# Readout of the first state space model: products over 128 rows first, products over 64 rows with the halves in turns

## The chip, the cores and the metric

The kernel runs on one core of one Trainium2 chip. The metric is the device time of one execution in microseconds (us); lower is better. The engines are TensorE (PE, with its weight loads shown as PEld), VectorE (DVE), ScalarE (ACT), GpSimd (POOL) and SyncE (SP), which issues most of the DMA transfers.

## The reference

Three blocks in a row on a sequence of 1024 positions with 1024 channels, all in f32: a block with stick-breaking attention and a convolution, a block with pooling and sliding-window attention, and a block with two state space models. The change lies in the third block, in the first of its two models (`s5_branch`): 64 groups of 16 channels, each with 64 complex states that decay independently.

```python
def step(h0, uc):
    bu = jnp.einsum('btgh,gnh->btgn', uc, B_bar)
    a = jnp.broadcast_to(A_bar, bu.shape)
    _, local = lax.associative_scan(combine, (a, bu), axis=1)
    states = local + pows * h0[:, None]
    y = jnp.einsum('btgn,ghn->btgh', states, Cc).real
    return states[:, -1], y
```

The output then gets `D * u` added, goes through a gelu, a gate by a projection of itself (`w_glu`) and a gate by `z_s5`, and is joined with the second model's output in `w_out`.

## The kernel before

Each engine has one program, written out in order; a small book of names turns `w.wait_ge(name, ...)` into waits on semaphores. Large products are made from f32 operands split into a high and a low part (`mm3`, lines 561 to 563, three products each). Their weights come in by SP (`load_raw`, line 3458), ScalarE makes the high part (L1218) and GpSimd the low part (L3214).

The first state space model takes 8 positions together, so that a sequence of 1024 is 128 chunks of 8. The work goes by eight blocks of 128 channels, e_ = 0 to 7 (called groups here). A block holds 8 groups of 16 channels of the reference. For each of them there is a table of 128x128 that gives the part of the output from the inputs of the same chunk, and two tables of 64x128 (real and imaginary part) that give the part from the state ahead of the chunk. The tables were made earlier, lie in DRAM, and are loaded into one of two places (`tab5`), even and odd blocks in turns.

PE's program per block, from `tensor_program`:

- `uproj(e_ + 1, e_, ...)`: the projection of the next block's inputs (L561 to L563), this block's gate projection, and the transposes (L567) that lay the next block's inputs out by chunk (`UG`).
- `results(e_)`, the readout, lines 1141 to 1155. Per half hf of the partitions it takes a PSUM bank of two (`ybk`), waits for the tables (`tab_s`, `tab_a`) and for the states (`h5`), and makes four tiles of 128 columns. Each tile is the sum of three products: the chunk's own inputs over 128 rows (L1152), the real part of the state over 64 rows (L1153) and the imaginary part over 64 rows (L1154). Half 0 uses partitions 0 to 63 of the states and their tables, half 1 partitions 64 to 127. Each half signals `y5_ps` at its end.
- `mid(e_ + 1)`: the inputs to the next block's states (L1137).
- `turned5(e_)`: transposes of the readout (L567).

Block 7 has its readout and its transposes later, behind the first quarter of the output projection (`wo(0, 0, 0)`), with nothing between them.

Who is waiting on the readout: ScalarE applies the gelu to each half's bank (`back5`, L2064), and the transposes wait for both. SP's `load_t(e_ + 2)` (L3629 for the tables, L3631 for four of the eight pieces of the 128x128 table) and ScalarE's (L1994, the other four) wait for `y5_ps` of half 1, since they load into the place that the readout has just used; SP issues the next weights behind that. `load_t(1)` alone is issued earlier, during block 0's projections. The states come from `mid` on VectorE and GpSimd: ScalarE copies L1137's result (L2057), VectorE multiplies (L3075 on), scans, and ends with L3101, which signals `h5`. ScalarE's L2006 evacuates the input projection; in ScalarE's program it stands behind an L1218.

Of the kernel before, what the change touches and what calls it, by code (L numbers as in the profile page):

```python
# [226 lines left out]
def build(nc, ap, out):  # L227
    ctx = ExitStack()
    with ctx:
# [4 lines left out]
        psum = ctx.enter_context(nc.psum_tensor("psum", [128, 8, 512], F32))  # L234
# [7 lines left out]
        def view(at, *shape):  # L242

            a = int(round(at * KB))
            n = 1
            for x in shape:
                n *= x
            v = arena[:, a:a + n]
            if len(shape) == 2:
                v = v.rearrange("p (a b) -> p a b", a=shape[0])  # L250
            elif len(shape) == 3:
                v = v.rearrange("p (a b c) -> p a b c", a=shape[0], b=shape[1])
            return v

        def half_of(half):
            return slice(512 * half, 512 * half + 512)

        def tile_of(tile):
            return slice(128 * tile, 128 * tile + 128)
# [257 lines left out]
        UG = [view(48, 8, 128), view(52, 8, 128)]  # L517
        Wr5, Wi5, Gr5, Gi5 = view(56, 4, 128), view(58, 4, 128), view(60, 4, 128), view(62, 4, 128)
        Hr5, Hi5, Xa5, Xb5 = view(64, 4, 128), view(66, 4, 128), view(68, 4, 128), view(70, 4, 128)
# [5 lines left out]
        def tab5(e_):  # L525

            a = T_AT[e_ % 2]
            t = view(a, 6, 4, 128)
            return [view(a, 8, 64), view(a + 2, 8, 64)], [t[:, q] for q in range(2, 6)], view(a + 12, 8, 128)
# [11 lines left out]
        def tensor_program(e, w):  # L541
# [4 lines left out]
            def take(ring, key, *freed):  # L546

                bank, before = ring.turn(*freed)
                book.bank_of[key] = bank
                for event in before:  # L550
                    w.wait_ge(*event)
                return bank
# [12 lines left out]
            def tp(o, in_):  # L565
                n = in_.shape[0]
                return e.transpose(o, in_, ident[0:n, 0:n])  # L567
# [301 lines left out]
            for g in range(4):  # L869
                run(proj_cm("u2_ps", (g,), w2, 256 * g, 2, pb, lambda m, half: [("u2", g, m, half)]))  # L870
                run(proj_cm("z2_ps", (2 * g,), w2, 4096 + 256 * g, 2, pb, lambda m, half: [("z2", 2 * g, m, half)]))
                for m in range(2):
                    for half in range(2):
                        bank = take(pb, ("pool_ps", g, m, half), ("pool", g, m, half))
# [3 lines left out]
                        for kb in range(2):  # L878
                            t = e.matmul(psum[:, bank, :], WP[:, kb, 128 * m:128 * m + 128], PL[:, kb, half_of(half)],  # L879
                                         start=kb == 0, stop=kb == 1)  # L880
# [17 lines left out]
            for m in range(8):  # L898
                run(proj_cm("q2_ps", (m,), w2, 128 * m, 1, pb, lambda _, half: [("q2", m, half)]))
                if m == 0:  # L900
                    for hf in range(2):
                        bank = take(pb, ("v2_tp", hf), ("v2", hf))
                        w.wait_ge("v2c", hf)
                        for j in range(4):
                            t = tp(psum[:, bank, tile_of(j)], V2T[:, tile_of(4 * hf + j)])
# [91 lines left out]
            for half in range(2):  # L997
                bank = take(pbk, ("dt_tp", half), ("dt_add", half))
                w.wait_ge("dt_c", half)
                for k in range(4):  # L1000
                    t = tp(psum[:, bank, tile_of(k)], DTF[half][:, tile_of(k)])
# [3 lines left out]
            bank = take(sb, ("dt_acs",), ("dt_dec_in",), ("dt_et",))  # L1005
# [77 lines left out]
            p5k, ubk, wbk, ybk = Banks(free_bank, [0, 1]), Banks(free_bank, [2, 3]), Banks(free_bank, [4, 5]), Banks(free_bank, [6, 7])  # L1083
# [56 lines left out]

            def results(e_):
                _, (car, cai, _, _), TG = tab5(e_)
                for hf in range(2):
                    lo = 64 * hf
                    bank = take(ybk, ("y5_ps", e_, hf), ("ys", e_, hf))
                    w.wait_ge("tab_s", e_)
                    w.wait_ge("tab_a", e_)
                    w.wait_ge("h5", e_)
                    w.wait_ge("h5_z", 1)
                    for k in range(4):  # L1150
                        ps = psum[:, bank, tile_of(k)]
                        e.matmul(ps, UG[e_ % 2][:, 2 * k + hf, :], TG[:, 2 * k + hf, :], start=True, stop=False)  # L1152
                        e.matmul(ps, Hr5[lo:lo + 64, k, :], car[lo:lo + 64, k, :], start=False, stop=False)  # L1153
                        t = e.matmul(ps, Hi5[lo:lo + 64, k, :], cai[lo:lo + 64, k, :], start=False, stop=True)  # L1154
                    t.then_inc(*w.up("y5_ps", e_, hf))

            def turned5(e_):
                for hf in range(2):
# [10 lines left out]
            for e_ in range(7):  # L1169
                uproj(e_ + 1, e_, lambda: e_ or step("sum", 3, 1, Banks(free_bank, [7])))  # L1170
                results(e_)
                mid(e_ + 1)
                turned5(e_)
# [5 lines left out]
            for half in range(2):  # L1179
                for ch in range(2):  # L1180
                    wo(0, half, ch, pb if half else Banks(free_bank, [2, 3, 6, 7] if ch else [0, 1, 4, 5]))
                    if half + ch == 0:
                        results(7)
                        turned5(7)
# [9 lines left out]
            for ch in range(2):  # L1194
                r = book.raw_of.get(("ple", ch), 0)
                wt = raw(r, 2, 512)
                for tile in range(8):
                    bank = take(pb, ("pp_ps", ch, tile), ("pp", ch, tile))
                    w.wait_ge("raw", r)
                    w.wait_ge("pt3")  # L1200
                    for kb in range(2):
                        t = e.matmul(psum[:, bank, :], PT3[:, kb, tile_of(tile)], wt[:, kb, :], start=kb == 0, stop=kb == 1)  # L1202
# [2572 lines left out]
```

## Time and profile before

| | |
|---|---|
| time, median of 3 runs | 3140.32 us (3138.95 to 3142.75) |
| span of the profiled execution, first to last instruction | 3139.1 us |
| PE busy | 3048.2 us (97%), 15412 instructions |
| DVE, ACT, POOL busy | 1650.6, 1155.6, 964.1 us |
| mean granted TensorE clock | 0.991 of full speed |

The profile is of one execution, and its times count from the span's start. Its span is 1.2 us below the median of the runs. PE's instructions overlap: the start of one to the start of the next says what it costs, its own duration includes what runs beneath its neighbours.

### The profile page before, as it was taken

The numbers are of one execution on the slowest core, as the hardware profiler recorded it, in microseconds if no ns is written. First come the engines' busy times: TensorE is split into PE (matmuls) and PEld (weight loads), VectorE is DVE, ScalarE is ACT, GpSimd is POOL, SyncE is SP. The second block draws the span as 40 slices with busy tenths as digits, with TensorE's granted clock in tenths as the row PEclk, the third lists the DMA queues.
The fourth block names the chain that finished last, engine by engine and source line by source line (L and its number), as shares of the span: only waits on it lengthen the run. The fifth ranks groups of instructions, "written<-read, shape, count | busy, mean of one in ns | idle before, by whom it ended". The sixth has DMA issues, their size and how long they took to land.

```text
span 3139.1 us, 38243 instructions
## 1 busy us (share of the span) xinstructions
PE 3048.2 (97%) x15412; PEld 2443.9 (78%) x15412; DVE 1650.6 (53%) x2710; ACT 1155.6 (37%) x1971; POOL 964.1 (31%) x700
## 2 busy tenths in 40 slices
PE   8999989999999999999999999999999999999998
PEld 7876658887878888777888756778778878788877
DVE  6989661025546654233243587666655555533436
ACT  3125553222341121113332286445546323332334
POOL 2220002233417785124522122411111233342523
PEclk9999989999999999999999999999999999999999
DMA  4110001112422233113332210421011243443323
GB/s 137 47 36 19 14 14 47 48 54 108 135 62 86 86 105 95 44 47 134 108 116 61 56 55 28 161 76 34 22 47 48 92 110 94 141 139 109 108 74 108
DMA packets 252657, 243.75 MB, mean 78 GB/s; under 512 B 15776, under 2 KB 198048, under 8 KB 251456
## 3 DMA queue, kind: packets, MB, share of 16 engines
q1 hardware_dynamic: 231536, 197.10, 21.0%
q10 hardware_dynamic: 20944, 44.21, 4.3%
q8 instruction: 122, 2.00, 0.3%
q14 instruction: 55, 0.45, 0.0%
HBM read 200.83 MB, written 38.73 MB: 76 GB/s over the span
## 4 chain that ended last, share of the span: by engine, by line
PE 84%; DVE 6%; ACT 4%; DMA 3%; issue 1%; POOL 1%; SPq 1%; ACTq 0%; DVEq 0%
PE psum L561 23%; PE psum L563 23%; PE psum L562 23%; PE psum L567 3%; DMA arena<-in_w_in 2%; PE psum L744 1%; PE psum L770 1%; DVE arena L2915 1%; PE psum L1202 1%; PE psum L1153 1%; PE psum L1152 1%; PE psum L934 1%; ACT WS L1218 1%; PE psum L879 1%; PE psum L958 1%
## 5 line engine op out<-in xcount | busy, mean ns | idle before, releaser
L3214 POOL TENSOR_TENSOR WS<-arena,WS 128x1024 fp32r<-128x1024 f32 x279 | 692.7, 2488 | 1729.2 <-ACT WS L1218 1729.1
L561 PE MATMUL psum<-XH,WS 128*128 128x512 f32 x2600 | 1031.9, 397 | 16.2 <-ACT arena L2006 3.5
L563 PE MATMUL psum<-XH,WS 128*128 128x512 f32 x2600 | 1015.6, 391 | 0.0
L562 PE MATMUL psum<-XL,WS 128*128 128x512 f32 x2600 | 1014.9, 390 | 0.0
L561 PEld LDWEIGHTS psum<-XH,WS 128*128 128x128 f32 x2600 | 489.2, 188 | 134.3 <-issue 13.8
L563 PEld LDWEIGHTS psum<-XH,WS 128*128 128x128 f32 x2600 | 489.0, 188 | 103.5
L562 PEld LDWEIGHTS psum<-XL,WS 128*128 128x128 f32 x2600 | 489.5, 188 | 96.7 <-issue 0.7
L1218 ACT ACTIVATE WS<-arena 128x1024 fp32r<-128x1024 f32 x279 | 293.0, 1059 | 730.9 <-PE psum L563 255.3
L561 PE MATMUL psum<-WS,XH 128*128 128x512 f32 x960 | 378.1, 394 | 7.2 <-POOL WS L3214 5.1
L562 PE MATMUL psum<-WS,XH 128*128 128x512 f32 x960 | 374.9, 391 | 0.0
L563 PE MATMUL psum<-WS,XL 128*128 128x512 f32 x960 | 374.8, 390 | 0.0
L561 PEld LDWEIGHTS psum<-WS,XH 128*128 128x128 f32 x960 | 180.7, 188 | 53.4 <-issue 7.4
L563 PEld LDWEIGHTS psum<-WS,XL 128*128 128x128 f32 x960 | 180.7, 188 | 37.8
L562 PEld LDWEIGHTS psum<-WS,XH 128*128 128x128 f32 x960 | 180.8, 188 | 36.8 <-issue 0.2
L2241 DVE TENSOR_TENSOR XL<-arena,XH 128x512 fp32r<-128x512 f32 x86 | 85.7, 1052 | 206.1 <-ACT XH L1271 206.1
L567 PE MATMUL psum<-arena 128*128 128x128 f32 x1152 | 164.1, 282 | 21.3 <-DVE arena L2817 9.5
L2331 DVE SCALAR_TENSOR_TENSOR arena<-arena 128x1024 f32<-128x1024 f32 x120 | 180.3, 1502 | 3.4
L567 PEld LDWEIGHTS psum<-arena 128*128 128x128 f32 x1152 | 132.8, 146 | 53.3 <-issue 29.0
L3298 POOL TENSOR_TENSOR arena<-arena 128x8 f32<-128x8 f32 (+7 forms) x320 | 153.9, 508 | 60.4 <-DVE arena L2549 52.9
L2549 DVE TENSOR_TENSOR arena<-arena 128x64 f32<-128x64 f32 (+5 forms) x188 | 115.0, 651 | 63.4 <-ACT arena L1605 32.2
L2376 DVE TENSOR_TENSOR_SCAN arena<-arena 128x128 f32<-128x128 f32 (+7 forms) x64 | 93.2, 1456 | 43.2 <-ACT arena L1407 43.1
L2915 DVE SCALAR_TENSOR_TENSOR arena<-arena 128x512 f32<-128x512 f32 x96 | 81.8, 852 | 51.9 <-ACT arena L1937 49.2
(304 smaller groups left out, 3075.2 us busy)
## 6 DMA issues: line engine op xcount, KB each, us to landing
arena<-in_w_in SPq DMA_DIRECT2D x85, 512.0 KB, 3.8
arena<-in_w_out SPq DMA_DIRECT2D x48, 512.0 KB, 3.5
arena<-in_w_in_even SPq DMA_DIRECT2D x48, 512.0 KB, 4.3
arena<-in_w_out_even SPq DMA_DIRECT2D x32, 512.0 KB, 3.6
h_spill<-arena ACTq DMA_DIRECT2D x24, 512.0 KB, 3.1
arena<-s_table SPq DMA_DIRECT2D x8, 1536.0 KB, 6.8
arena<-in_w_in_odd SPq DMA_DIRECT2D x18, 512.0 KB, 3.9
s_table<-arena SPq DMA_DIRECT2D x32, 256.0 KB, 3.0
```

Of the source, the lines that this page charges most:

```text
L561: e.matmul(ps, wh, xh, start=start, stop=False)
L562: e.matmul(ps, wh, xl, start=False, stop=False)
L563: return e.matmul(ps, wl, xh, start=False, stop=stop)
L567: return e.transpose(o, in_, ident[0:n, 0:n])
L1218: e.activation(split_hl(u, kbs, n)[0], raw(r, kbs, n), ACT.Copy).then_inc(*w.up("w_hi", u))
L2241: e.tensor_tensor(XL[:, kb, half_of(half)], src(kb)[:, half_of(half)], XH[:, kb, half_of(half)].bitcast(F32), SUB).then_inc(*w.up("x_lo_v" ...
L2331: e.scalar_tensor_tensor(o, c[:, k:k + S], col("conv_w", 31 * m + k), o, M, A_).then_inc(*w.up("conv", m, k))
L2376: e.tensor_tensor_scan(q[:, ::-1], q[:, ::-1], zero.broadcast_to([128, nk]), 1.0, M, A_).then_inc(*w.up("att_scan", k, h))
L2549: e.tensor_tensor(o, a, b, op).then_inc(*w.up("tbv", *key, also=also))
L2915: e.scalar_tensor_tensor(o, R[:, k:k + 512], col("conv_w_3", 16 * k + cb), o, M, A_).then_inc(*w.up("cv_k", g, i, half, k, also=[("cv_c", ...
L3214: e.tensor_tensor(lo, raw(book.raw_of.get(("w", u), 0), kbs, n), hi.bitcast(F32), SUB).then_inc(*w.up("w_lo", u))
L3298: e.tensor_tensor(o, a, b, op).then_inc(*w.up("tbp", *key, also=also))
```

## The change

In the readout, both banks are taken at the start, and the eight products over 128 rows of both halves come first, waiting only for the tables. Of the products in a bank the first alone carries `start`. Then come the wait for the states and the sixteen products over 64 rows: per tile, first the real and then the imaginary part, each for half 0 and half 1 in turn. Both halves signal at the end, with the last two products. The number and the operands of the products are as before.

```diff
             def results(e_):
                 _, (car, cai, _, _), TG = tab5(e_)
+                banks = [take(ybk, ("y5_ps", e_, hf), ("ys", e_, hf)) for hf in range(2)]
+                w.wait_ge("tab_s", e_)
+                w.wait_ge("tab_a", e_)
                 for hf in range(2):
-                    lo = 64 * hf
-                    bank = take(ybk, ("y5_ps", e_, hf), ("ys", e_, hf))
-                    w.wait_ge("tab_s", e_)
-                    w.wait_ge("tab_a", e_)
-                    w.wait_ge("h5", e_)
-                    w.wait_ge("h5_z", 1)
                     for k in range(4):
-                        ps = psum[:, bank, tile_of(k)]
-                        e.matmul(ps, UG[e_ % 2][:, 2 * k + hf, :], TG[:, 2 * k + hf, :], start=True, stop=False)
-                        e.matmul(ps, Hr5[lo:lo + 64, k, :], car[lo:lo + 64, k, :], start=False, stop=False)
-                        t = e.matmul(ps, Hi5[lo:lo + 64, k, :], cai[lo:lo + 64, k, :], start=False, stop=True)
-                    t.then_inc(*w.up("y5_ps", e_, hf))
+                        e.matmul(psum[:, banks[hf], tile_of(k)], UG[e_ % 2][:, 2 * k + hf, :], TG[:, 2 * k + hf, :],
+                                 start=k == 0, stop=False)
+                w.wait_ge("h5", e_)
+                w.wait_ge("h5_z", 1)
+                for k in range(4):
+                    for h, ca in ((Hr5, car), (Hi5, cai)):
+                        for hf in range(2):
+                            lo, last = slice(64 * hf, 64 * hf + 64), k == 3 and h is Hi5
+                            t = e.matmul(psum[:, banks[hf], tile_of(k)], h[lo, k, :], ca[lo, k, :], start=False, stop=last)
+                            if last:
+                                t.then_inc(*w.up("y5_ps", e_, hf))
```

## Rows read from the trace of the kernel before

**Rows 1.** The page's chain that ended last, shares of the span by engine.

```profile
PE 84%; DVE 6%; ACT 4%; DMA 3%; issue 1%; POOL 1%; SPq 1%; ACTq 0%; DVEq 0%
```

**Rows 2.** Groups by line and form: count, busy us, mean ns, idle before.

```profile
L1153 PE MATMUL psum<-arena 64*128 64x128 f32 x128 | 31.1, 323 | 0.0
```

**Rows 3.** Timeline of PE, first readout: start us, duration us, instructions merged by line.

```profile
2494.35 1.03 PE L567 MATMUL psum<-arena 128*128 128x128 f32 x8
2495.22 0.39 PE L1152 MATMUL psum<-arena 128*128 128x128 f32 x2
2495.54 0.49 PE L1153 MATMUL psum<-arena 64*128 64x128 f32 x2
2495.86 0.39 PE L1154 MATMUL psum<-arena 64*128 64x128 f32 x2
2496.18 0.49 PE L1152 MATMUL psum<-arena 128*128 128x128 f32 x2
2496.60 0.48 PE L1153 MATMUL psum<-arena 64*128 64x128 f32 x2
...
2503.57 1.97 PE L1137 MATMUL psum<-arena 128*64 128x128 f32 x32
```

**Rows 4.** Chain of waits behind the third readout: start us, share of the chain, what.

```profile
2576.07 0.55 SPq L3631
...
2578.85 9.36 DMA arena<-in_w_in
...
2589.83 0.50 PE psum L561
```

**Rows 5.** Timelines of VectorE and of PE ahead of the third readout.

```profile
2557.51 2.87 DVE L3101 TENSOR_TENSOR arena<-arena 128x508 f32<-128x508 f32 x1
...
2566.38 1.03 PE L567 MATMUL psum<-arena 128*128 128x128 f32 x8
```

**Rows 6.** Timeline of PE, attention scores of the second block, halves in turns.

```profile
1795.84 1.16 PE L934 MATMUL psum<-arena 64*128 64x128 f32 x16
1796.93 0.50 PE L561 MATMUL psum<-XH,WS 128*128 128x512 f32 x1
...
1798.52 0.71 PE L934 MATMUL psum<-arena 64*128 64x128 f32 x8
```

**Rows 7.** Timeline of PE, making of the tables, halves in turns, 16-column weights.

```profile
961.66 1.92 PE L853 MATMUL psum<-arena 64*16 64x128 f32 x32
```

**Rows 8.** Table of group 1: last issue in SP's timeline; that issue's time to landing.

```profile
2493.46 0.61 SPq L3631 DMA_DIRECT2D arena<-k_table  x1
...
DMA to landing us min/median/max: 8.9/8.9/8.9
```

**Rows 9.** Timeline of PE, first half of the gate projection after the first readout.

```profile
2518.72 0.50 PE L561 MATMUL psum<-XH,WS 128*128 128x512 f32 x1 [1.25 <-ACT arena L2006]
```

**Rows 10.** PE timeline, then two stretches: engines' busy us, granted clock, DMA share, GB/s.

```profile
2739.19 0.50 PE L561 MATMUL psum<-WS,XH 128*128 128x512 f32 x1 [2.31 <-POOL WS L3214]
...
2740.80:2744.10 3.30, 3.30 (x10) 2.56 (x9) 1.66 (x1) 1.06 (x1) 1.55 (x2) 0.50 0.68 219
960.00:1215.00 255.00, 254.88 (x1334) 208.81 (x1333) 143.99 (x174) 48.35 (x71) 200.51 (x350) 1.00 0.33 96
```

**Rows 11.** Timeline of ScalarE around the first readout.

```profile
2499.72 0.60 ACT L2064 ACTIVATE arena<-psum 128x512 f32<-128x512 f32 x1
2503.68 0.60 ACT L2064 ACTIVATE arena<-psum 128x512 f32<-128x512 f32 x1 [3.37 <-PE psum L1154]
2504.71 0.60 ACT L2057 ACTIVATE arena<-psum 128x512 f32<-128x512 f32 x1 [0.44 <-PE psum L1137]
```

**Rows 12.** Timelines of PE and ScalarE, readout of group 7.

```profile
2757.26 0.38 PE L1152 MATMUL psum<-arena 128*128 128x128 f32 x2
2766.45 1.06 PE L567 MATMUL psum<-arena 128*128 128x128 f32 x8 [0.78 <-ACT arena L2064]
...
2765.71 0.60 ACT L2064 ACTIVATE arena<-psum 128x512 f32<-128x512 f32 x1 [3.63 <-PE psum L1154]
```

## The prediction

> **What bounds the kernel now.** I read the page first. TensorE (PE) makes up 84% of the chain that ended last [rows 1], so the question is what the change does to PE's own time. Line 1153, one of the two 64-row lines that the change touches, has 128 matrix instructions [rows 2]: 8 groups with 8 products each and two instructions to a product. The code gives lines 1152 and 1154 as many.
>
> Then the timeline of PE for the first readout [rows 3]. The readout runs from 2495.22 to 2503.57, when the next group's L1137 begins: 8.35 us for 24 products, 0.35 us each. The transposes ahead of it, which have the same 128x128x128 shape, start every (2495.22 - 2494.35) / 8 = 0.109 us an instruction, so 0.22 us a product. The excess sits where the row count changes: the two instructions of L1152 take 0.32 us up to L1153 (0.42 in the second round, 2496.18 to 2496.60), L1153 takes 0.32 and L1154 0.32, though the two lines of 64 rows do each no more than half of the work of L1152. PE does not stand idle in there; it is slow between forms.
>
> Does the readout lie on the path? The chain of waits in the loop over groups says yes: when a readout ends, SP issues the tables and weights for later groups, the weights land 9.36 us after their issue, and PE's second projection half begins at 2589.83 behind them [rows 4]. All of that starts at the readout's end, as does PE's own next work. The other input of a readout, the state from VectorE, is early: its last operation ends at 2557.51 + 2.87 = 2560.38, the readout starts at 2566.38 + 8 x 0.109 = 2567.25 [rows 5]. Both hang on the previous readout's end by unchanged work, so these 6.9 us of slack stay. Moving the wait for that state behind the 8 full products therefore gains nothing and costs nothing.
>
> **The change part by part.** The 8 full products together: 16 instructions x 0.109 [rows 3] = 1.74 us. Entering the 64-row form once: 0.32 - 0.22 = 0.10 us [rows 3].
>
> The 16 products of 64 rows, now with the two halves in turns into two banks: the trace of before has this pattern in the attention scores of the second block, same 64x128 weights and 128 columns [rows 6]. There 16 instructions begin at 1795.84 and the next form begins at 1796.93, so 1.09 us with the way out included; a block of 8 lasts 0.71 and one of 16 lasts 1.16, so 8 more cost 0.45 (0.056 each, about half of 0.109). For 32 instructions: 1.09 + 2 x 0.45 = 1.99 us. Bounds: the same alternation with 16-column weights and with sums of two products as here runs 32 instructions in 1.92 us [rows 7], last duration included, where my price gives 1.16 + 0.90 = 2.06: 0.14 less at the cheap end. At the dear end the halves don't overlap and each instruction takes 0.109 as a full one does: 32 x 0.109 + 0.2 = 3.7 us. I take 1.99, since its rows agree in shape. Sending `start` once per bank instead of four times changes a flag; L1152 (with it, first round) and L1154 (without) both take 0.32 [rows 3], so zero. Taking both banks ahead waits for the second gelu of the group before, which ended before that group's transposes.
>
> New readout: 1.74 + 0.10 + 1.99 = 3.83 us, a gain of 8.35 - 3.83 = **4.52 us** each (4.66 to 2.8 by the bounds). Six of the eight, groups 1 to 6, give this in full: 27.1 us. The other two don't.
>
> Group 0. After its readout PE runs L1137 of group 1, which needs that group's table. The last piece is issued by SP at 2493.46 and lands 8.9 us later [rows 8], at 2502.36, and its issue does not depend on the readout. Now L1137 starts at 2503.57 and never waits; after the change PE would be there at 2495.22 + 3.83 = 2499.05 and waits till about 2502.5: 1.07 us of the 4.52 remain. Behind the waiting L1137 on PE stand group 0's transposes and the next projection, which move with it; ScalarE's copies and the chain of group 1's states begin with it too and keep their slack to the next readout. The wait then relieves another: in this round PE waited 1.25 us for an evacuation that stood behind the weights' landing [rows 9], and those weights are asked for up to 4.5 us earlier (less, as the queue is still full). I take the whole 1.2; 0 is the other end. Against it stands the clock: after PE's idle stretch of 2.31 us before 2739.19 the granted clock was 0.50 from 2740.80 to 2744.10 [rows 10], half of full speed (1.2 GHz), which costs half of 3.30, 1.65 us. The new wait of 3.2 us is longer, so I charge 1.5 (0 to 3.3, two such stretches). Group 0 nets 1.07 + 1.2 - 1.5 = 0.8 us (-2.2 to 2.3).
>
> Evacuation. Both banks now finish together, where the first gelu used to run beneath the second half [rows 11]. A gelu takes 0.60 us. In groups 0 to 6 two in a row (1.2 us) fit beneath L1137, whose 32 instructions last 1.97 us [rows 3], so the transposes behind them are not held up; the copy of L2057 would begin at 2503.68 + 1.2 = 2504.88 in place of 2504.71, inside the 6.9 us of slack. In group 7 nothing lies between: the transposes began at 2766.45, right behind the second gelu of 2765.71 [rows 12]. New: 2757.26 + 1.74 + 0.10 + 2.06 = 2761.16, two gelus to 2762.40, transposes at 2762.54 (the 0.14 of before kept). Gain 3.9 us instead of 4.5.
>
> The Trainium skill (TensorEngine Tiling, PSUM Bottleneck) says that tiling speeds up the products but not the emptying of the banks, which may become the limit. If that held for every group, 0.6 us more would be lost in seven of them, 4.2 us in all, an estimate from the page's rule and the gelu's row. The rows side with it for group 7 alone.
>
> Sum: 27.1 + 0.8 + 3.9 = **31.8 us**. The span of the profiled execution is 3139.1, and 3107.3 would be left. The median of the runs, 3140.3, stands 1.2 above that span, so the prediction is 3108.5 us. Whether the half-clock stretch at 2740.80 comes again after the shift is open, 1.65 us either way.
>
> **Rivals.**
> No overlap, only fewer changes of form: the halves go one after the other at 0.109. Readout 1.74 + 0.10 + 3.7 = 5.5, gain 2.8: 6 x 2.8 = 16.8, group 7 some 2.2, group 0 some 2.3 (its wait is then 1.7 us and I charge no clock), 21 us, **3119 us**. Against it stand both blocks in turns [rows 6, 7]. Chance 0.07.
>
> Each change of half costs what a change of form costs, so the edit does not do what it says: 32 instructions at 0.21, the pace of L1152 behind a change in [rows 3] (0.42 for two), give 6.7; readout 1.74 + 0.10 + 6.7 + 0.2 = 8.7, about 0.4 more than before; with the late gelu of group 7 some 4 us in all, **3144 us**. The attention scores speak against it [rows 6]. The Trainium skill (TensorEngine Tiling, Key Properties) says that a change of tiling mode drains the engine and a change of tile alone does not; by that rule this case is out, and the trace agrees (0.056 us an instruction [rows 6]). Chance 0.05.
>
> Slower: the clock. With half of the rows active in short blocks the chip could count the readout as rest and grant half clock behind it, in each group. An instruction's time doubles, so half of the stretch is lost; the 4.0 us that a group gains on average are gone once the half clock lasts 8 us a group. At twice that, 16 us, it costs 8 - 4 = 4 us a group, 32 in all: **3172 us**. For it: clock drops of 3.3 us exist [rows 10]. Against it: in the 255 us that hold all eight table blocks of 64 rows in turns the granted clock is 1.00 [rows 10]. Chance 0.03.
>
> **How the numbers follow.** The forecast has 0.85; its own range is 3104 (all of group 0's relief, no clock loss, no drop at 2740) to 3113 (group 0 at its worst, a dearer pair). The full range, 3103 to 3117, leaves out the three rivals and some of the forecast's tails, together under 0.2. A difference of 0.2%, 6.3 us, is about what a measurement of this kernel can tell from none. Faster by more: forecast and first rival, 0.92. Within: the second rival, 0.05. Slower: 0.03.
>
> **What would show it.** Right: the 8 full products some 1.7 us in a row, 32 instructions of 64 rows in pairs over some 2.0 us, a readout of 3.8 in groups 1 to 6; in group 0 PE idle ahead of L1137 for about 3 us, released by a table load; in group 7 two gelus one behind the other and PE waiting about 1.3 us for them. Wrong: pairs that don't overlap; the round of a group shortened by less than its readout, with a new PE wait behind a weight load or the state; a granted clock below 1.00 in groups 1 to 6.

## Result and the profile after

The changed kernel takes 3111.26 us (median of 4 runs, 3107.21 to 3113.56) against 3140.76 beside it: ratio 0.9904, 95% interval 0.9892 to 0.9916. Run again beside three of the experiments it took 3107.43 us, ratio 0.9892 (0.9875 to 0.9908). Forecast were 3108.5 us, 3103 to 3117.

The span of the profiled execution is 3108.1 us, 31.0 less than before. PE still makes up most of the chain that ended last. DMA and SP, which stood in the chain of the group loop before [rows 4], have shrunk in it, from 3% to 2% (DMA) and from 1% to 0% (SPq). The page's chain, by engine:

```profile
PE 85%; DVE 7%; ACT 4%; DMA 2%; issue 1%; POOL 1%; SPq 0%; ACTq 0%; DVEq 0%
```

The readout of group 1, in PE's timeline (start us, duration us, instructions merged by line; L1148 is the full product, L1156 the 64-row product, L1137 the next group's first work):

```profile
2532.02 1.95 PE L1148 MATMUL psum<-arena 128*128 128x128 f32 x16
2533.90 2.06 PE L1156 MATMUL psum<-arena 64*128 64x128 f32 x32
2535.89 1.97 PE L1137 MATMUL psum<-arena 128*64 128x128 f32 x32
2537.78 1.09 PE L567 MATMUL psum<-arena 128*128 128x128 f32 x8
```

It takes 2535.89 - 2532.02 = 3.87 us where it took 8.35 [rows 3]; the groups 1 to 6 all have this within 0.01. The 32 instructions of 64 rows last 2.06 us, to the hundredth what was worked out from the attention scores [rows 6].

Group 0, PE's timeline again:

```profile
2496.36 1.03 PE L567 MATMUL psum<-arena 128*128 128x128 f32 x8
2497.23 1.95 PE L1148 MATMUL psum<-arena 128*128 128x128 f32 x16
2499.11 2.06 PE L1156 MATMUL psum<-arena 64*128 64x128 f32 x32
2504.06 3.50 PE L1137 MATMUL psum<-arena 128*64 128x128 f32 x32 [2.89 <-issue]
2507.49 1.09 PE L567 MATMUL psum<-arena 128*128 128x128 f32 x8
```

PE stands idle for 2.89 us ahead of L1137. The profile names no engine as releaser ("issue"), but the last piece of group 1's table, issued at 2495.50 (2495.5 in the line's summary below), lands 8.5 us later, so at 2504.0, and L1137 starts at 2504.06:

```profile
L3634 SPq DMA_DIRECT2D arena<-k_table x1: 599/599/599, 2495.5 to 2495.5; - x1
...
DMA to landing us min/median/max: 8.5/8.5/8.5
```

L1137 then takes 2507.49 - 2504.06 = 3.43 us and not 1.89 as in group 1, because its stretch has the granted clock at half (0.50, the number behind the engines' busy times; the stretch after it has 1.00):

```profile
2504.00:2507.20 3.20, 3.14 (x30) 3.17 (x32) 0.00 (x0) 0.60 (x1) 0.00 (x0) 0.50 1.03 321
2507.30:2524.00 16.70, 16.70 (x82) 13.85 (x79) 14.25 (x18) 4.97 (x6) 10.33 (x6) 1.00 0.67 128
```

Group 7, timelines of PE and of ScalarE (L2067 is the gelu):

```profile
2730.17 1.95 PE L1148 MATMUL psum<-arena 128*128 128x128 f32 x16
2732.05 2.06 PE L1156 MATMUL psum<-arena 64*128 64x128 f32 x32
2735.36 1.06 PE L567 MATMUL psum<-arena 128*128 128x128 f32 x8 [1.26 <-ACT arena L2067]
...
2734.13 1.08 ACT L2067 ACTIVATE arena<-psum 128x512 f32<-128x512 f32 x2 [0.98 <-PE psum L1156]
```

Both gelus now run one behind the other after the readout, and PE waits 1.26 us for them where it waited 0.78 [rows 12]. From the readout's start to the transposes it is 2735.36 - 2730.17 = 5.19 us, 9.19 before.

All waits of PE in the stage, from 2495 to 2740 (waiter, releaser: us in total, times, longest):

```profile
PE psum L1137 <- issue: 2.9, 1, 2.9
PE psum L561 <- POOL WS L3217: 2.3, 1, 2.3
PE psum L561 <- ACT arena L2009: 2.2, 2, 1.6
PE psum L567 <- ACT arena L2067: 1.3, 1, 1.3
PE psum L561 <- DVE arena L3112: 0.8, 1, 0.8
```

The first is the new one. The wait on ScalarE's evacuation (L2009, L2006 before) fell from 3.5 us in six times to 2.2 in two; the 1.25 us of group 0's round [rows 9] are gone.

Where the time went, by starts of the readouts in the two traces: the round of group 0 (first readout to second) 36.35 to 34.79 us, a gain of 1.6; the six rounds of groups 1 to 6 (second readout to the last) 225.7 to 198.2, 27.5; from the last readout on 4.0. Together 33.1 us. The first readout of the profiled execution after begins 2.0 us later than before (2497.23 against 2495.22): 1.2 us of that are there within the first 16 us, the rest comes in later stages, none of which the change touches; hence 31.0 in the spans.

### The profile page after: what moved, and what is told of

The parts are those of the page before. It is cut to its first block, busy times and chain, and to the rows that moved or that the text cites. A ratio compares the mean times of both kernels' runs of the same rounds, so it can differ in the third digit from the quotient of the medians.

```text
span 3108.1 us, 38242 instructions
## 1 busy us (share of the span) xinstructions
PE 3014.0 (97%) x15412; PEld 2423.2 (78%) x15412; DVE 1649.9 (53%) x2710; ACT 1154.8 (37%) x1971; POOL 962.6 (31%) x700
## 4 chain that ended last, share of the span: by engine, by line
PE 85%; DVE 7%; ACT 4%; DMA 2%; issue 1%; POOL 1%; SPq 0%; ACTq 0%; DVEq 0%
PE psum L561 24%; PE psum L563 23%; PE psum L562 23%; PE psum L567 4%; PE psum L744 1%; PE psum L770 1%; DVE arena L2918 1%; DMA arena<-in_w_in 1%; PE psum L1205 1%; PE psum L934 1%; PE psum L879 1%; PE psum L958 1%; PE psum L750 1%; ACT WS L1221 1%; PE psum L1025 1%
```

## The experiments

A change of form, below, is a step from products over 128 rows to products over 64 rows or back. The first three kernels are set beside the trace of the changed kernel from the result; the changed kernel was not timed again beside them.

**Halves in a row: the turns taken out.** The changed kernel with the loops exchanged.

```diff
-                for k in range(4):
-                    for h, ca in ((Hr5, car), (Hi5, cai)):
-                        for hf in range(2):
+                for hf in range(2):
+                    for k in range(4):
+                        for h, ca in ((Hr5, car), (Hi5, cai)):
```

> The changed kernel, but the 64-row products go half after half (eight of half 0, then eight of half 1), so that no two halves stand in turns; the full products still come first. Both causes: a change of form costs about 0.2 us and a 64-row instruction without its partner of the other half takes 0.109 us in place of 0.056. Then the readout takes 1.88 + 32 x 0.11 + 0.2 = 5.6 us in groups 1 to 6 where the changed kernel has 3.87, and the whole is about 11 us slower than the changed kernel, some 3122 us (group 0 gets its clock back). Rival, fewer changes of form are everything (0.28 us each): readout 3.9 us, no difference. Rival, the turns are everything and changes of form cost nothing: readout 8.3 us, about 27 us slower, as the kernel before.

Measured: 3117.75 us, ratio 0.9926 (0.9910 to 0.9943). PE's timeline of group 1's readout:

```profile
2533.45 1.95 PE L1148 MATMUL psum<-arena 128*128 128x128 f32 x16
2535.33 3.50 PE L1156 MATMUL psum<-arena 64*128 64x128 f32 x32
2538.76 1.97 PE L1137 MATMUL psum<-arena 128*64 128x128 f32 x32
```

2538.76 - 2533.45 = 5.31 us, so neither rival holds: without turns 8.35 - 5.31 = 3.04 us of the gain are there, and the turns bring 5.31 - 3.87 = 1.44 us more. The 5.6 expected were 0.3 too many, and the seam, where half 0 ends and half 1 begins, shows why. The counts below are the 64-row matrix instructions that run in a stretch ahead of the seam, across it and behind it (busy and count of PE, of PEld, then granted clock, DMA share, GB/s):

```profile
2535.40:2536.70 1.30, 1.30 (x12) 1.30 (x13) 1.00 0.00 0
2536.70:2537.20 0.50, 0.50 (x10) 0.50 (x9) 1.00 0.00 0
2537.20:2538.50 1.30, 1.30 (x16) 1.30 (x13) 1.00 0.06 13
```

An instruction lasts 0.27 us and starts every 0.112 here, so a stretch of 0.50 us would touch (0.50 + 0.27) / 0.112, about 7; it touches 10. About three instructions of half 1 run beside the last ones of half 0: the engine begins on half 1 before all of half 0 has started. In the trace's own starts the instruction that signals the end of half 0, the 16th of the block in the program, is the 19th to start. This overlap is worth 3 x 0.112 = 0.3 us and belongs to the turns, so that about 2.7 us of the 4.48 come from fewer changes of form and about 1.8 from running the halves beside each other.

From the first readout to the end this kernel takes 619.1 us where the changed kernel has 610.8: 8.3 us more, about 11 expected. One part of what was expected did not come: group 0 does not get its clock back. PE idles for 1.40 us ahead of L1137, and the clock behind it is half again (last row, columns as above for all five engines):

```profile
2505.41 3.07 PE L1137 MATMUL psum<-arena 128*64 128x128 f32 x32 [1.40 <-issue]
...
2506.20:2509.40 3.20, 3.20 (x27) 2.87 (x24) 0.09 (x1) 1.20 (x2) 0.00 (x0) 0.50 1.01 360
```

**A change of form per tile: the full products not ahead.** The turns stay, the two full products go back to their tile.

```diff
-                for hf in range(2):
-                    for k in range(4):
-                        e.matmul(psum[:, banks[hf], tile_of(k)], UG[e_ % 2][:, 2 * k + hf, :], TG[:, 2 * k + hf, :],
-                                 start=k == 0, stop=False)
                 w.wait_ge("h5", e_)
                 w.wait_ge("h5_z", 1)
                 for k in range(4):
+                    for hf in range(2):
+                        e.matmul(psum[:, banks[hf], tile_of(k)], UG[e_ % 2][:, 2 * k + hf, :], TG[:, 2 * k + hf, :],
+                                 start=k == 0, stop=False)
```

> The halves in turns as in the changed kernel, but the full products not ahead: per tile two full products, then four of 64 rows in turns, so eight changes of form in place of two. Both causes: 16 x 0.109 + 32 x 0.056 + 8 x 0.2 = 5.1 us a readout, 1.25 us more than the changed kernel, some 7 to 9 us slower, about 3119 us. Rival, changes of form are everything (0.28 each): 5.6 us. Rival, the turns are everything: 3.9 us, no difference.

Measured: 3117.40 us, ratio 0.9927 (0.9913 to 0.9942). PE's timeline, the first two of four rounds and the end:

```profile
2533.94 0.61 PE L1150 MATMUL psum<-arena 128*128 128x128 f32 x4
2534.48 0.71 PE L1155 MATMUL psum<-arena 64*128 64x128 f32 x8
2535.12 0.71 PE L1150 MATMUL psum<-arena 128*128 128x128 f32 x4
2535.77 0.71 PE L1155 MATMUL psum<-arena 64*128 64x128 f32 x8
...
2538.99 1.97 PE L1137 MATMUL psum<-arena 128*64 128x128 f32 x32
```

The readout takes 5.05 us, 5.1 expected. Six changes of form more than in the changed kernel cost 5.05 - 3.87 = 1.18 us, 0.20 each. At that price the 14 changes by which the kernel before exceeds the changed one make 2.8 us, beside the 2.7 found above. A block of four full instructions takes 0.65 us (2535.12 to 2535.77) where 4 x 0.112 = 0.45 would do: the price is paid at the edges of each block, as read ahead of the change [rows 3]. Two other readings of it fall away. It is not the `start` flag, which is sent here as in the changed kernel; and it is not the adding of one product after another into the same tile, which the halves in a row do for real and imaginary part at 0.112 us an instruction.

From the first readout to the end it takes 618.7 us, 7.9 more than the changed kernel, 7 to 9 expected. In group 0 PE idles for 1.31 us ahead of L1137, and here the clock behind it stays at 1.00:

```profile
2507.20 1.97 PE L1137 MATMUL psum<-arena 128*64 128x128 f32 x32 [1.31 <-issue]
...
2507.20:2510.40 3.20, 3.20 (x42) 2.99 (x43) 0.40 (x1) 1.20 (x2) 0.08 (x1) 1.00 1.06 361
```

**Turns of two products.** The loops over `hf` and over the real and imaginary part exchanged.

```diff
-                    for h, ca in ((Hr5, car), (Hi5, cai)):
-                        for hf in range(2):
+                    for hf in range(2):
+                        for h, ca in ((Hr5, car), (Hi5, cai)):
```

> The changed kernel with the halves in turns of two products (real and imaginary part of half 0, then of half 1). If an instruction overlaps only with the one that stands right beside it, seven of the boundaries pair: about 0.7 us saved against the 5.6 us of halves in a row, readout 4.9 us. If the engine looks past the next product to the other half, the pairs stay and the readout takes 3.9 us, no difference to the changed kernel (3111 us).

Measured: 3109.67 us (two runs), ratio 0.9902 (0.9882 to 0.9922).

```profile
2530.85 1.95 PE L1148 MATMUL psum<-arena 128*128 128x128 f32 x16
2532.73 2.16 PE L1156 MATMUL psum<-arena 64*128 64x128 f32 x32
2534.82 1.97 PE L1137 MATMUL psum<-arena 128*64 128x128 f32 x32
```

The readout takes 3.97 us, 3.9 expected for an engine that looks past the next product; the block lasts 2.16 us where the changed kernel has 2.06. So turns of two pair as well as turns of one but for 0.1 us. With the seam above (about three instructions in a block of 16) that bounds the reach here: two products yes, eight no.

**The changed kernel again**, unedited, beside the three experiments that follow.

> The changed kernel itself, timed beside the next three on one chip. 3111 us, group 0's L1137 waiting 2.9 us for its table and half clock for 3.4 us behind it.

Measured: 3107.43 us (3106.76 to 3108.42), ratio 0.9892 (0.9875 to 0.9908). The readouts take 3.87 us again, and the wait ahead of L1137 in group 0 comes again with half clock behind it (the row from 2502.70 in the next experiment).

**Table ahead of the store.** In SP's program, the table of group 1 ahead of the last store of the second model.

```diff
                         store_y(2)
-                        store_y(3)
+                        for k in range(2):
+                            w.wait_ge("y_nrm", 3, k)
                         load_t(1)
+                        store_y(3)
```

> The changed kernel, with the table of group 1 issued ahead of the store of the last group of the second model (y_spill, 1 MB) in SP's queue, not behind it. If the new wait in group 0 is for the table's landing behind that store, the table lands some 2 us earlier, the wait falls from 2.9 to about 1 us, and the half-clock stretch of 3.4 us behind it (1.5 us) goes with it: 2 to 3.5 us faster than the changed kernel. Rival, the store isn't what holds the table (the issue of its pieces is): wait and time as in the changed kernel. Rival, the clock drop doesn't come from the wait: the wait shrinks and the half clock stays.

Measured: 3108.35 us (3106.09 to 3109.64), the changed kernel beside it 3107.43 (3106.76 to 3108.42): by time, nothing, where 2 to 3.5 us were expected. By trace the step does what it should. The pieces of the table land 6.4 to 7.2 us after their issue, not 8.5 as the last one in the changed kernel, and L1137 doesn't wait at all (1 us was expected to remain):

```profile
2500.99 2.06 PE L1156 MATMUL psum<-arena 64*128 64x128 f32 x32
2503.01 1.97 PE L1137 MATMUL psum<-arena 128*64 128x128 f32 x32
2505.30 1.06 PE L567 MATMUL psum<-arena 128*128 128x128 f32 x8 [0.31 <-ACT arena L2067]
```

Group 0's round takes 31.94 us where the changed kernel beside it has 34.75: 2.8 gained. The granted clock there is 1.00. But this execution has half clock in two other stretches, which the changed kernel's execution beside it does not have. First this kernel, then the changed one, same columns as above with all five engines:

```profile
2502.50:2505.90 3.40, 3.09 (x48) 2.74 (x47) 0.00 (x0) 3.12 (x5) 0.00 (x0) 1.00 1.15 388
2711.60:2714.60 3.00, 3.00 (x9) 2.35 (x8) 2.12 (x1) 0.94 (x1) 1.57 (x1) 0.50 0.57 188
2735.50:2738.50 3.00, 2.91 (x7) 2.36 (x8) 2.59 (x4) 0.00 (x0) 0.00 (x0) 0.50 0.35 97
```

```profile
2502.70:2505.80 3.10, 3.02 (x29) 3.04 (x31) 0.00 (x0) 0.60 (x1) 0.00 (x0) 0.50 1.08 318
2711.60:2714.60 3.00, 2.85 (x12) 2.37 (x13) 3.00 (x2) 0.00 (x0) 2.91 (x2) 1.00 0.55 174
2735.50:2738.50 3.00, 2.66 (x12) 2.23 (x13) 2.89 (x5) 0.00 (x0) 0.00 (x0) 1.00 0.33 111
```

One stretch at half clock is gone, two of the same length have come, each behind an idle stretch that both kernels have (2.3 us near 2709, and 1.3 to 1.8 us with 0.8 behind it near 2733). By starts of the readouts, beside the changed kernel's execution, group 0 gains 2.8 us and the five rounds behind it 1.6 (153.9 against 155.5); the round of group 6, with the first of the two stretches, loses 1.6 (43.6 against 42.0), and the rest, with the second, 0.9. From the first readout to the end 1.9 us remain (608.7 against 610.6), too little to be told in the times. In this execution they are not even to be seen in the span, which is 1.2 us longer than the changed kernel's: its first readout begins 3.1 us later (2499.11 against 2496.00), in stages ahead of the edit that spent longer at half clock (from 2200 to 2340 the mean granted clock is 0.93, against 0.95). Whether the edit alone is worth anything in the median stays open; the next experiment but one speaks for it.

**Weights ahead of the tables.** In SP's loop over groups:

```diff
                 if e_ < 6:
+                    ws.ahead(2)
                     load_t(e_ + 2)
```

> The changed kernel, with each group's two weight loads issued on SP ahead of the tables of the group after next, not behind them. If the waits of PE on ScalarE's evacuation (L2009 in the changed kernel, 2.2 us in all) come from weights that land behind the tables, they go: about 2 us faster than the changed kernel. Rival, with the readout shorter the rounds hang on that chain and more comes out, up to 4 us. Rival, the tables land later and make a new wait: slower.

Measured: 3106.78 us (3104.37 to 3109.61), 0.65 under the changed kernel beside it, with ranges that overlap: small or nothing by time. The trace: around the third readout the weights land 4.8 to 5.9 us after their issue and no longer 10.3 to 11.1, as in the first trace of the changed kernel, and the wait on the evacuation is gone from the list of PE's waits:

```profile
PE psum L1137 <- issue: 2.4, 1, 2.4
PE psum L561 <- POOL WS L3217: 2.3, 1, 2.3
PE psum L567 <- ACT arena L2067: 1.3, 1, 1.3
PE psum L561 <- DVE arena L3112: 0.8, 1, 0.8
```

All five rounds from group 1 to group 6 take 30.28 us; beside it the changed kernel's take 30.66 to 31.55. So the evacuation's wait did come from weights behind tables, and with it gone a round is PE's own work alone. The tables' issue waits for the end of the readout, so weights ahead of it also start earlier: around the third readout at 2560.32, and at 2569.04 in the changed kernel beside it. How much comes from the earlier start and how much from the shorter landing is not taken apart.

The five rounds together gain 4.1 us (151.4 against 155.5), the 4 us of the first rival and not the 2 expected. The round of group 6 loses 1.6 of it (43.6 against 42.0), again to a stretch at half clock (0.50 from 2707 to 2710) that the changed kernel beside it does not have; group 0 keeps its wait and its half clock. From the first readout to the end 3.4 us remain (607.3 against 610.6).

**Both.** The two edits together.

> Both of the two preceding edits together. If their causes are separate the gains add: 4 to 5.5 us faster than the changed kernel, about 3106 us. If the weights ahead delay group 1's table again, less.

Measured: 3100.90 us (3098.90 to 3101.93), ratio 0.9871 (0.9856 to 0.9886). That is 6.5 us under the changed kernel beside it, somewhat more than the 4 to 5.5 expected, and the four times of the one lie below all four of the other. PE's waits in the stage:

```profile
PE psum L561 <- POOL WS L3217: 2.3, 1, 2.3
PE psum L567 <- ACT arena L2067: 1.6, 2, 1.3
PE psum L561 <- DVE arena L3112: 0.8, 1, 0.8
```

From the first readout to the end it takes 603.5 us where the changed kernel beside it has 610.6: group 0's round gains 4.1 us (30.7 against 34.8), the five rounds behind it 4.1, the round of group 6 loses 1.6 to half clock as above, and the rest gains 0.6. It is the fastest version of this study, and beats both kernels.

## Why the prediction was right

*The readout.* Forecast 3.83 us, measured 3.87. The price of the block in turns held to the hundredth; the missing 0.04 is the full products, which go at 0.112 us an instruction and not at the transposes' 0.109. That the gain has two sources is now shown apart: about 2.7 us from fewer changes of form and 1.8 from the turns, so the larger part comes from moving the full products ahead. The Trainium skill (TensorEngine Tiling, Key Properties) says that changing the tiling mode, and not just the tile, drains TensorE. The trace agrees in the prices, 0.20 us for each change of form and none for the turns; a drain as such it does not show.

*Six groups in full.* Forecast 27.1 us, measured 27.5 for their rounds: 6 x 4.48 = 26.9 from the readouts, the rest from smaller waits that I have not taken apart. No new wait for the state or for weights came up.

*Group 0.* Forecast 0.8 us, measured 1.6; the one term clearly off, and inside its range. The wait for the table came as worked out (2.89 us idle, 3.2 forecast); measured from the start of the transposes ahead of the readout, L1137 comes 9.22 us later before [rows 3] and 7.70 after, so 1.52 of the gain remained and not 1.07, most of it because the table landed 8.5 us after its issue and not 8.9. The half clock cost 3.43 - 1.89 = 1.54 us, 1.5 charged. The relief of the next waits was 1.6 us, 1.2 forecast: from L1137 to the second readout it is 27.96 us after and 28.00 before, with the 1.54 of half clock in the one. The half clock never comes there without the wait (before, table ahead, both edits together: 1.00). With it, it came behind 2.4 to 2.9 us (the changed kernel twice, turns of two, the weights alone ahead) and behind 1.40 (halves in a row), but not behind 1.31 (a change of form per tile). So the 1.5 us charged were a likely price and not a sure one.

*Group 7.* Forecast 3.9 us, measured 4.0, with both gelus in the open as said. (Two gelus of 0.60 us behind 2761.16 end at 2762.36 and not at 2762.40; the slip changes nothing.) The remark of the Trainium skill on emptying the banks (TensorEngine Tiling, PSUM Bottleneck) holds for this group alone, as its rows had it: in groups 0 to 6 no wait for a gelu appears in the list above. That is partly because group 0 waited for its table: with the table ahead of the store, its transposes wait 0.31 us for a gelu (the row from 2505.30 there), so there two gelus do not quite fit beneath L1137.

*The sum.* Forecast 31.8 us; 29.5 by the medians of the first comparison, 33.7 by those of the second, 33.1 by the trace from the first readout on.

*The rivals.* No overlap: the halves in a row show about what it would have been, 5.31 us a readout and 3118 us in all (5.6 without the overlap at the seam). Its group 0 was priced without half clock, and that kernel had it. Each change of half as dear as a change of form: out, by the block's 2.06 us. Half clock behind every readout: out. Behind the readouts of groups 1 to 6 the clock stays at 1.00; the stage has one new stretch at half clock, behind group 0's wait, and the one of before at 2740.80 came again, at 2712, though not in the second trace of the changed kernel (1.00 from 2711.60).

## What to carry to other kernels

Look at PE's timeline by starts, not by idle time: the profile showed PE fully busy in the readout, while every change between products over 128 and over 64 rows cost 0.20 us. Put products of one form together, and products over 64 rows so that the halves of the partitions take turns into different banks; a price for such a block can be read from any other block of the same shape in the trace. When a stage gets shorter, look for the transfer whose issue does not move with it: it may be the next wait, and the clock behind that wait can be part of its price.

## What was not expected

The engine starts matrix instructions of the other half ahead of their place in the program: turns of two products cost only 0.1 us more than turns of one (2.16 against 2.06 us), and even two blocks of eight products overlap by about three instructions at their seam.

Stretches at half clock come and go between executions and kernels behind the same idle gaps. Here a stretch of some 3 us costs about 1.6 us. The changed kernel with group 1's table ahead shows none at 2503 but two later on, in the one execution that was profiled, and a gain of 2.8 us in one round and 1.6 in those behind it did not appear in its times. Together with the weights ahead it did: 6.5 us, where the two medians alone gave +0.9 and -0.7. That half clock hid the gains in the other executions too is likely, but not shown, since each of these versions has one trace.
